# Block-diagonal 128-row products in the chunk scan of a hybrid layer: one matmul for both heads of a pair

## The reference, cut to what matters

```python
t_inv = lax.linalg.triangular_solve(lower + eye, eye, left_side=True, lower=True, unit_diagonal=True)
value = jnp.einsum('bnhij,bnhjd->bnhid', t_inv, v * beta[..., None])
k_cum = jnp.einsum('bnhij,bnhjd->bnhid', t_inv, k_beta * jnp.exp(gc)[..., None])
def step(s, inp):                       # lax.scan over the 16 chunks
    q_i, val_i, kc_i, at_i, gl_i, kt_i = inp
    v_new = val_i - jnp.einsum('bhcd,bhde->bhce', kc_i, s)
    o = jnp.einsum('bhcd,bhde->bhce', q_i, s) + jnp.einsum('bhij,bhje->bhie', at_i, v_new)
    s = s * jnp.exp(gl_i)[..., None, None] + jnp.einsum('bhcd,bhce->bhde', kt_i, v_new)
    return s, o
```

## Time and profile before

| | |
|---|---|
| time, median of 3 runs | 2027.59 us (2026.8 to 2030.23) |
| the profiled execution | 2032.76 us, span 2031.0 us |
| PE busy | 1942.1 us, 96% |
| DVE, ACT, POOL busy | 1051.2, 568.6, 552.0 us |
| the scan | about 789.5 to 995 us of the span |

### The profile page before, as it was taken

The page is one execution under the profiler, slowest core; times in us unless marked ns, Lnnn a source line. Parts: engine busy times, 40 slices in busy tenths (PEclk is TensorE's granted clock), DMA queues, the critical chain, the costliest instruction groups (busy, mean ns, idle before and its releaser), DMA issues.

```text
span 2031.0 us, 29371 instructions
## 1 busy us (share of the span) xinstructions
PE 1942.1 (96%) x11744; PEld 1570.1 (77%) x11744; DVE 1051.2 (52%) x1379; ACT 568.6 (28%) x888; POOL 552.0 (27%) x336
## 2 busy tenths in 40 slices
PE   8999999999999998989799999999999999999994
PEld 7777787677788887777677777788888888888883
DVE  3747643764379402877677428334343424242437
ACT  3445423334211112444421312221212121221112
POOL 1211212211123223444243734321212121212203
PEclk9999999999999998999899999999999999999997
DMA  6435672345642762766363630321212121212102
GB/s 160 66 97 129 166 183 60 83 117 151 161 127 84 164 206 96 209 197 193 131 202 99 212 108 20 92 62 31 62 31 62 31 62 31 62 31 62 39 13 83
DMA packets 339846, 211.85 MB, mean 104 GB/s; under 512 B 166140, under 2 KB 310140, under 8 KB 337696
## 3 DMA queue, kind: packets, MB, share of 16 engines
q1 hardware_dynamic: 264176, 156.38, 27.9%
q10 hardware_dynamic: 75568, 54.04, 9.2%
HBM read 151.27 MB, written 59.06 MB: 104 GB/s over the span
## 4 chain that ended last, share of the span: by engine, by line
PE 45%; DVE 3%; POOL 2%; DMA 0%; issue 0%; ACT 0%; SPq 0%; DVEq 0%; ACTq 0%
PE b_ps L154 11%; PE b_ps L155 11%; PE b_ps L156 11%; PE f_ps L154 4%; PE f_ps L155 4%; PE f_ps L156 4%; POOL x1lo L1763 1%; DVE l_stats L2276 1%; PE f_ps L1844 1%; DMA o_raw<-in_w_out 0%; DVE y L2288 0%; DVE y L2273 0%; POOL wo_lo L1769 0%; PE f_ps L1881 0%; PE f_ps L1806 0%; POOL x1lo L1755 0%
## 5 line engine op out<-in xcount | busy, mean ns | idle before, releaser
L154 PE MATMUL bank<-xhi,w_hi 128*128 128x512 f32 x976 | 393.3, 403 | 0.5 <-DVE xlo L938 0.5
L156 PE MATMUL bank<-xhi,w_lo 128*128 128x512 f32 x976 | 385.9, 395 | 0.0
L155 PE MATMUL bank<-xlo,w_hi 128*128 128x512 f32 x976 | 385.9, 395 | 0.0
L433 POOL TENSOR_TENSOR w_lo<-w_raw,w_hi 128x1024 fp32r<-128x1024 f32 x61 | 167.4, 2744 | 600.1 <-ACT w_hi L799 600.1
L2248 DVE TENSOR_TENSOR bw_raw<-bw_raw,b_ps 128x512 f32<-128x512 f32 x42 | 28.9, 687 | 388.4 <-PE b_ps L156 380.1
L154 PEld LDWEIGHTS bank<-xhi,w_hi 128*128 128x128 f32 x976 | 183.8, 188 | 45.9 <-issue 3.7
L156 PEld LDWEIGHTS bank<-xhi,w_lo 128*128 128x128 f32 x976 | 183.4, 188 | 44.6
L155 PEld LDWEIGHTS bank<-xlo,w_hi 128*128 128x128 f32 x976 | 183.6, 188 | 44.0 <-issue 1.8
L2256 DVE TENSOR_TENSOR y<-y,f_ps 128x512 f32<-128x512 f32 x320 | 200.5, 683 | 0.5
L1791 POOL TENSOR_TENSOR bw_split<-ff_raw_down,ff_hi_down 128x1024 fp32r<-128x1024 f32 x22 | 53.3, 2423 | 526.7 <-ACT ff_hi_down L2049 526.7
L154 PE MATMUL f_ps<-ff_hi_down,ff_hhi 128*128 128x512 f32 x352 | 142.7, 405 | 3.6 <-DVE ff_hlo L2267 3.6
(11 more groups left out here) (325 smaller groups left out, 3463.8 us busy)
## 6 DMA issues: line engine op xcount, KB each, us to landing
w_raw<-in_w_in ACTq DMA_DIRECT2D x61, 512.0 KB, 4.3
op<-opnd SPq DMA_DIRECT2D x16, 1152.0 KB, 5.5
u<-work ACTq DMA_DIRECT2D x68, 256.0 KB, 3.5
b_gate<-u SPq DMA_DIRECT2D x24, 512.0 KB, 3.5
ff_raw_gate<-in_ffn_gate SPq DMA_DIRECT2D x22, 512.0 KB, 4.0
ff_raw_up<-in_ffn_up SPq DMA_DIRECT2D x22, 512.0 KB, 5.3
ff_raw_down<-in_ffn_down SPq DMA_DIRECT2D x22, 512.0 KB, 5.8
opnd<-work SPq DMA_DIRECT2D x20, 512.0 KB, 5.8
```

The lines of the kernel that those rows point to most:

```text
L154: pe.matmul(out, w_hi, x_hi, start=first, stop=False)
L155: pe.matmul(out, w_hi, x_lo, start=False, stop=False)
L156: return pe.matmul(out, w_lo, x_hi, start=False, stop=last)
L433: pool.tensor_tensor(w_lo[b][:, :, :], w_raw[b][:, :, :], as_f32(w_hi[b][:, :, :]), ALU.subtract).then_inc(w_lo_done, 1)
```

## The change

The tiles `inv` and `corner` go, with the copies of `place_inverse`. `join` becomes 128 rows by 128 columns for each pair, three deep, cleared once before the scan; the DMA puts the two corners straight into it. `packed` (32 columns) is used as it landed. `y`, `z` and `w` become one matmul for each pair with all 128 rows and 128 columns of the array: 6 each, moving 32 columns (`y`, `z`) or 64 and 128 (`w`). `zt` is padded to 128 columns: GpSimd writes the left half of each head's block (`tensor_scalar` by a 0/1 column), VectorE the right half from `packed` and the product. The clearing of `join` is now waited for by SyncE before the first loads.

On VectorE `r_tmp` and `r_g` become two fused instructions; `VECTOR_TURNS` puts `s_g` behind the softmax denominator, `sv` right behind `s_g`, and `zt` last. ScalarE takes over the multiplication by the reciprocal, as four instructions of 128 columns, and TensorE's transposes wait for each of them apart.

```diff
 def load_chunk(sp, c, tiles, opnd, xinv, landed, inv_landed):
...
     for k in (0, 64):
-        sp.dma_start(corner[b][k:k + 32, :, :], xinv[c, k:k + 32, 2]).then_inc(inv_landed, 16)
+        sp.dma_start(join[b][k:k + NB, :, k + NB:k + 2 * NB], xinv[c, k:k + 32, 2]).then_inc(inv_landed, 16)
...
+VECTOR_TURNS = ("state", "attend", "product", "attend", "state", "product", "attend", "state", "attend", "state", "product", "attend")
...
@@ TensorE, product
-                if c:
-                    pe.wait_ge(zt_done, c)
...
-                pe.wait_ge(join_done, c * 2 + 2)
-                pe.wait_ge(inv_done, c * 4 + 4)
+                pe.wait_ge(inv_landed[d], c // DEEP * 48 + 48)
                 for u in range(NPAIR):
-                    for e in range(2):
-                        h = rwkv_rows(e)
-                        last = pe.matmul(ps_y[h, u, :], join[b][h, u, :], inv[b][h, 0, u, :], start=True, stop=True)
+                    last = pe.matmul(ps_y[:, u, :], join[d][:, u, :], packed[d][:, 0, u, :], start=True, stop=True)
...
-                pe.wait_ge(y_done, c + 1)
+                pe.wait_ge(y_done, c * 2 + 2)
                 pe.wait_ge(vt_done, c + 1)
+                if c:
+                    pe.wait_ge(zt_done, c * 2)
                 for u in range(NPAIR):
-                    for e in range(2):
-                        h = rwkv_rows(e)
-                        last = pe.matmul(ps_z[h, u, :], y[b][h, u, :], inv[b][h, 1, u, :], start=True, stop=True)
+                    last = pe.matmul(ps_z[:, u, :], y[b][:, u, :], packed[d][:, 1, u, :], start=True, stop=True)
...
@@ TensorE, state
-                pe.wait_ge(zt_done, c + 1)
+                pe.wait_ge(zt_done, c * 2 + 2)
+                pe.wait_ge(inv_done, c * 2 + 2)
                 pe.wait_ge(r_rw_done, c + 1)
                 for j in range(4):
-                    for e in range(2):
-                        h = rwkv_rows(e)
-                        pe.matmul(ps_w[h, j * C:(j + 1) * C], zt[b][h, j, :], r_rw[b][h, j, :], start=True, stop=True)
+                    pe.matmul(ps_w[:, j * C:(j + 1) * C], zt[b][:, j, :], r_rw[b][:, j, :], start=True, stop=True)
...
@@ VectorE
+                for e in range(2):
+                    h = rwkv_rows(e)
+                    dve.scalar_tensor_tensor(zt[b][h, :, lower_of(e)], packed[d][h, 1, :, :], tab("lower")[h, :], ps_z[h, :, :],
+                                             ALU.mult, ALU.add).then_inc(zt_done, 1)
...
+                for p in range(2):
+                    dve.scalar_tensor_tensor(r_g[b][:, p, :], ps_r[:, 256 + p * GD:256 + (p + 1) * GD], cols[:, c, 2, p:p + 1],
+                                             tok_g[b][:, 1, p, :], ALU.mult, ALU.add).then_inc(r_g_done, 1)
...
-                dve.wait_ge(rested, 2 * c + 2)
-                dve.tensor_tensor(score[b][:, :, :], score[b][:, :, :], rest[b][:, :].unsqueeze(2).to_broadcast([P, 4, W]), ALU.mult).then_inc(p_done, 1)
...
@@ ScalarE
-                act.activation(y[b][:, :, :], ps_y, ACT.Copy).then_inc(y_done, 1)
+                for e in range(2):
+                    act.activation(y[b][lower_of(e), :, 64 * e:64 * e + NB], ps_y[lower_of(e), :, :], ACT.Copy).then_inc(y_done, 1)
...
-                act.wait_ge(r_tmp_done, c + 1)
+                act.wait_ge(r_g_done, c * 2 + 2)
...
+                act.wait_ge(rested, 2 * c + 2)
+                for j in range(4):
+                    act.activation(score[b][:, j, :], score[b][:, j, :], ACT.Copy, scale=rest[b][:, j:j + 1]).then_inc(p_done, 1)
...
@@ GpSimd
-                if c:
-                    place_inverse(pool, c, tiles, join_done, inv_done)
-                pool.wait_ge(inv_done, c * 4 + 4)
+                if c >= 2:
+                    pool.wait_ge(mm_w, c - 1)
+                for e in range(2):
+                    h = rwkv_rows(e)
+                    pool.tensor_scalar(zt[b][h, :, 64 * e:64 * e + NB], packed[d][h, 1, :, :], tab("upper")[h, :], None, ALU.mult).then_inc(inv_done, 1)
+                pool.wait_ge(inv_done, c * 2 + 2)
```

More of the change, by code:

```diff
@@ L78, in constants @@
     put("causal_again", t >= s)
+    put("upper", s < 32)
+    put("lower", s >= 32)
     put("corner", (s < 32) & (t >= 32))
@@ L259, in scan_tiles @@
     op, ar, sv, wv = loads("op", [N_FLAT]), loads("ar", [8, 2, C]), loads("sv", [8, C]), loads("wv", [8, C])
-    packed, corner = loads("inv_packed", [2, NPAIR, NB]), loads("inv_corner", [NPAIR, NB])
-    inv, join = ([sb(f"{name}{b}", [P] + shape) for b in range(2)] for name, shape in (("inv", [2, NPAIR, C]), ("join", [NPAIR, C])))
-    return op, ar, sv, wv, packed, corner, inv, join
+    packed, join = loads("inv_packed", [2, NPAIR, NB]), loads("join", [NPAIR, P])
+    return op, ar, sv, wv, packed, join
 def load_chunk(sp, c, tiles, opnd, xinv, landed, inv_landed):
-    op, ar, sv, wv, packed, corner, inv, join = tiles
+    op, ar, sv, wv, packed, join = tiles
     b, row = c % DEEP, opnd[c]
@@ L434, in _ @@
             local.sweep(pool)
-            *_, inv, join = early
+            *_, join = early
             pool.wait_ge(inv_stored, 16 * 4 * R)
-            for b in range(2):
-                pool.memset(inv[b][:, :, :, :], 0.0).then_inc(early_cleared, 1)
+            for b in range(DEEP):
                 pool.memset(join[b][:, :, :], 0.0).then_inc(early_cleared, 1)
[L440 to L443, removed]
+            pool.wait_ge(early_cleared, DEEP)
         @block.sync
@@ L588, in _ @@
                 sp.wait_ge(turn_stored[b], 16 * turn_count[b])
+            sp.wait_ge(early_cleared, DEEP)
             for c in range(DEEP):
@@ L1148, in scan_and_attend @@
         local.enter_context(nc.sbuf_tensor("scan_tiles", [P, sum(math.prod(t.shape[1:]) for group in tiles for t in group)], F32))
-        op, ar, sv, wv, packed, corner, inv, join = tiles
+        op, ar, sv, wv, packed, join = tiles
         causal, attn = two("causal", [8, C]), two("attn", [2, 2, C])
         tok_g = two("tok_g", [2, 2, GD])
-        y, zt = two("y", [NPAIR, C]), two("zt", [NPAIR, C])
-        r_rw, r_g, r_tmp, w_g = two("r_rw", [4, C]), two("r_g", [2, GD]), two("r_tmp", [2, GD]), two("w_g", [2 * GD])
+        y, zt = two("y", [NPAIR, P]), two("zt", [NPAIR, P])
+        r_rw, r_g, w_g = two("r_rw", [4, C]), two("r_g", [2, GD]), two("w_g", [2 * GD])
         s_g, s_dec, s_sum = two("s_g", [GH, GD]), two("s_dec", [GH, GD]), two("s_sum", [4, C])
@@ L1188, in scan_and_attend, with run @@
         of = lambda e: slice(4 * e, 4 * e + 4)
-        def run(product, state, attend):
+        def run(product, state, attend, turns):
             first = product(0)
@@ L1359, in sum_values @@
                 last.then_inc(mm_pv, 1)
-            run(product, state, attend)
+            run(product, state, attend, TURNS)
             sum_values(NCH - 1)
@@ L1550, in state @@
                 yield
-            run(product, state, lambda c: iter(()))
+            run(product, state, lambda c: iter(()), TURNS)
             local.sweep(pool)
```

61 lines of the change are left out of this document (28 added, 33 removed).

## The result

| | before | after |
|---|---|---|
| time, median | 2028.37 us | 2048.4 us (2046.15 to 2052.47, 4 runs) |
| the profiled execution | 2032.76, span 2031.0 | 2046.15, span 2044.4 |

The change makes the kernel slower: ratio 1.0101, 95% interval 1.0081 to 1.012. I had forecast slower, by 7 us, with a range up to 2042. It is 20 us by the medians. One execution of the 256-byte version in experiment 7 ran at a granted clock of 0.748 and took 2412.3 us; no ratio here uses it.

What follows compares the result with a forecast made beforehand. TensorE, busy 96%, was taken as the bound, with a 1.40 us wait per chunk. 15 steps of +0.48 us (row +1.88, wait -1.40) gave +7.2, edges +0.3; taken as +7, 2034 us, range 2013 to 2042.

Steps and rivals of the forecast that it cites:

- The step that failed: Ahead of the scan: clearing `join` before the loads delays SyncE a few us at most, within its 42.1 us wait.
- what costs nothing: List of side changes taken as free: fused `r_tmp` and `r_g`, `zt` last, GpSimd's work, `join`'s DMA and its clearing.
- The distance of the passes: TensorE's `y`, `z`, `w`: 128-column weight loads set the spacing, 0.12 us a pass, bounds 0.056 and 0.15.
- The chunk: One scan chunk: TensorE's row +1.88 us, the removed wait -1.40, so +0.48 us a step.
- The wait of 1.40 us: TensorE's transposes waiting for VectorE's multiplication in every chunk; the whole 1.40 us was to go.
- `sv`: VectorE behind `s_g`: one half held by `s_dec` until 8.95, cost taken as 0, at most some 0.3 us a chunk.
- The edges: First and last chunks of the scan: +2.2 - 1.9 - 0.5 + 0.5 = +0.3 us.
- The 1 us that was to come back: First chunk: about 1 us of the half-clock cost of `y` and `z` returns, as later groups run after the clock rises.
- The last step: Step from chunk 14 to 15, 13.92 us before: -1.9 us, as `sv` comes ahead of GpSimd's last splits.
- A: Rival at the `y`, `z`, `w` passes: spacing at the break-even 0.107 us, change pays nothing, about 2028; chance 0.24.
- B: Rival at `y`, `z`, `w`: passes limited by 32 columns or half-width loads, 0.056 us, faster, about 2013; chance 0.21.
- C: Rival: second half of `r` waits 0.5 us a chunk, about 2042, or loads and columns don't overlap, about 2045; chance 0.13.

Runs made afterwards that it cites:

- experiment 7: Kernel before with 8 bytes more in the constant table, 2032.9 us, or 256 bytes more, 2028.66; changed kernel with small tiles, early Exp, columns in `corner`, 2014.51.
- experiment 1: The changed kernel, but VectorE clears the `join` tiles in place of GpSimd: 2041.0 us, ratio 1.007.
- experiment 2: The kernel before with one wait more, SyncE waiting for GpSimd's four clears before the first loads: 2039.07 us, ratio 1.0048.
- experiment 8: The changed kernel, wide products kept, with VectorE clearing, one early Exp and the 0/1 columns in the mask `corner`: 2031.29 us, ratio 1.0019.
- experiment 5: The kernel of experiment 1 with `y`, `z`, `w` as one 64-column matmul per head, on 64 rows (2021.01 us) or 128 rows (2021.45 us).

## Why the prediction was wrong

**The step that failed.** "Clearing `join` before the loads delays SyncE by a few us at most ..., where it stood waiting 42.1 us." It stands under what costs nothing, and it put the cost at zero. I made two errors in it. I priced the clearing by its own length and not by its place in GpSimd's queue: its 2.1 us were right, but it can't start before the last `w_lo`, at 771 us. And I took a wait that SyncE has behind the loads as room for a wait ahead of them. The loads went from 711 to 773 us, the wait for the first `m` from 3.6 to 13.6 us: 7.4 us by experiment 1, 10.7 by experiment 2. I should have read which instruction waits for the 42.1 us, and what it stands behind: it is L595, which comes after all three sets of loads and waits for the stores of `u`. No rival had this mechanism in it, so the range did not cover it either.

**What no step named.** The 8 bytes of the table, for which the kernel before pays 4 us with all else kept (2032.9 against 2028.6, and against 2028.7 with 256 bytes more), and the load of the Exp table, which the new order brings onto the chain of the first chunk (+1.2 us in the first step; the old order hid it). Of the 20 us, the clearing gives back 7.4, these two together 9.7, and 3.5 stay. By themselves the early Exp gave 1.7 and 4.2 us and the address 2.3 and 4.3, in sum 4.0 to 8.5, so 1 us or more of the 9.7 has no shown cause.

**The distance of the passes.** I took 0.12 us from the earlier trace rows; `y`, `z` and `w` show (1.42 - 0.19) / 11 = 0.112 us, (0.97 - 0.19) / 7 = 0.111 and (0.53 - 0.19) / 3 = 0.113. It doesn't depend on what moves: 32, 64 or 128 columns. The mechanism, that the load is the limit, was right, and 36 passes were 0.29 us a chunk dearer in the forecast than on the chip. The Trainium skill (TensorE: Matmul & The Clock Gate, section LDWEIGHTS) has the load's time set by its columns and not by its rows, 107 ns for 128 of them as an estimate by the page; the runs show 112 ns, and the two versions of experiment 5 agree on the rows. By the columns alone 64 would be half as long; the 64-column loads here come 0.028 us apart, a quarter of 0.112. What makes the other half was not tried.

**The chunk.** Forecast +0.48 us, measured +0.18. On TensorE's row `y` +0.62, `z` +0.61, `w` and the transposed values +0.09, scores +0.20 (the change of shape moved there): +1.52, against my +1.88. The wait of 1.40 us gave only 1.23, because a change of tile shape of 0.17 us was inside its bracket, and is there after. The second half of `r` gave 0.16 more, a wait for `sv` that was in its 0.54 us before. That makes +1.52 - 1.23 - 0.16 = +0.13, beside +0.18 by the steps. Two terms were off by 0.2 to 0.4 us and in opposite directions.

**`sv`.** I had put one half as held for the length of one `s_dec` and ending at the cost of nothing. VectorE and GpSimd in the chunk above, and `sv` over 815 to 960 us (duration ns min/median/max):

```profile
862.25 1.60 DVE L1407 TENSOR_TENSOR sv<-s_sum,plast 64x256 f32<-64x256 f32 x2
...
862.48 1.09 POOL L1542 TENSOR_TENSOR s_dec<-s_g,egl_bc 128x512 f32<-128x512 f32 x1 [8.17 <-DVE s_g L1400]
...
L1407 DVE TENSOR_TENSOR sv<-s_sum,plast x24: 408/786/1164, 826.0 to 959.9; 64x256 f32<-64x256 f32 x24
```

In each pair one takes 0.41 us and the other 1.16: it ends at 863.85, 0.28 us after `s_dec`, and `r`'s second half starts at 864.08 with no bracket. This step was right. So was that `rest` falls to 0.16 us, and that ScalarE's four multiplications (1.28 us, done at 862.87) come before the transposes at 863.11.

**The edges.** The first chunk: +3.1 us from `m` to `w` against the forecast +2.2 in all, and by other terms. `y` and `z` at the lower level of the clock (1.2 GHz; 0.50 in the window of 798 to 816 us) cost +1.62 and +1.20 where I had +1.6 each. The 1 us that was to come back didn't: the first `m` started at that level already, after the long wait, and took 1.79 us where before it had taken 1.06, and the groups before `w` took 0.88 us more. Shorter waits for `at_values` and `join` gave 1.35 back. Before, the first `m` was:

```profile
789.45 1.06 PEld L1241 LDWEIGHTS ps_m<-ar,op 64*128 64x128 f32 x16 [3.62 <-SPq L1215]
```

The last step fell from 13.88 to 11.80 us: -2.08 for a forecast -1.9. Before had two steps of 12.42 and 13.14 us; after has none like these, which I had not foreseen (-1.6). They are no fixed part of the kernel before: in other traces of its products in its order there was one of 12.15, one of 13.25 or two of 12.7 and 12.8, so that the steps come out even is in part luck. That is how 13 steps at +0.18, the first at +1.38 and these come to nothing.

**The rivals.** A (passes at the break-even) named the nearest distance, 0.112 for its 0.107, and by experiment 8 the time without the three mishaps is 2031, between A and the forecast. That is no merit of A: it had the time at 2028 and the distance as a break-even, and the size of the loss, 20 us, came from no rival. B's 0.056 us is excluded by the passes. C's waits of `r` did not come in the usual step. The direction was right, and it stays so without the three (experiment 8, +3.5 us). The reason for most of the 20 us was not in the prediction.

## What to carry to other kernels

Price an instruction that others must wait for by where it stands in its engine's queue, and a wait by what is queued behind it: a clearing of 2.1 us delayed loads by 62 us and the kernel by 7 to 11. Follow the delay to the engine that counts: TensorE waited for the third set of loads in a row, not for the one that it needed first. Count the stationary operand's columns before you merge small products: here two 64-column loads were half as dear as one of 128. When a change has two parts, run each alone: here the order wins 19 us by itself and the products with their tiles and constants lose 22. And compare the addresses of the tiles when a constant is added.

## What the runs showed of the hardware that was not expected

- A float32 weight load of 128 columns spaces its passes by 0.112 us, whether 32, 64 or 128 columns move behind it. 64-column loads come 0.028 us apart, with 64 rows (24 in 0.78 us) or 128 rows (24 in 0.78 us).
- Tiles moved by 8 bytes: 183 in place of 246 GB/s in the same 17 us, and 4 us more in all; moved by 256 bytes: 245 GB/s and no loss. Which of the moved tiles matters was not tried.
- A change of tile shape shows as a bracket of 0.17 us ahead of the first load, and hides inside a longer wait at the same place.
